# Second block's heads woven into a whole-fp32 projection, phase tables on VectorE in quarters, one order of products for both mixers

## The reference

```python
def first_block(...):                       # DEPTH = 2
    for l in range(DEPTH):
        h = rmsnorm(x, norm_mix[l])
        (u_ssm, q_lat, kv_lat, k_rope, hg_q, hg_f, hg_i, hg_g, gate_logits) = split(h @ w_in[l])
        y_ssm = s5_mixer(u_ssm, ...)        # complex state space scan: exp(lam*step)^t, B, C, gelu, GLU
        y_mla = mla_mixer(q_lat, kv_lat, k_rope, ...)
        y_hg  = hgrn2_mixer(hg_q, hg_f, hg_i, hg_g, ...)
        x = x + (gates[0]*y_ssm + gates[1]*y_mla + gates[2]*y_hg) @ w_out[l]
        x = x + memory_cross_attention(rmsnorm(x), rmsnorm(mem), ...)
        x = x + swiglu_ffn(rmsnorm(x), ...)
    return rmsnorm(x, norm_final)

def second_block(x, ...):                   # DEPTH = 2
    for l in range(DEPTH):
        h = rmsnorm_2(x, g_attn[l])
        qa, ka, va, qb, kb, vb = split(h @ w_in[l])      # w_in: 1024 x 2304
        qa, ka, qb, kb = rope(rmsnorm_2(each head))      # heads of 64
        ya = windowed_gqa_sink(qa, ka, va, sink[l])      # 8 heads, |distance| <= 128, a sink logit each
        yb = diff_attention(qb, kb, vb, lam)             # 4 heads: softmax(1) - lam * softmax(2)
        yb = rmsnorm_2(yb, subln[l]) * (1.0 - lambda_init)
        x = x + concat([ya, yb]) @ w_out[l]
        gate, val = split(rmsnorm_2(x, g_ffn[l]) @ w_up[l])
        x = x + (silu(conv3(gate)) * val) @ w_down[l]
    return x
```

## Time and profile before

| | us |
|---|---|
| median of three runs (2083.47 to 2090.02) | 2086.99 |
| the profiled execution, its own time | 2090.09 |
| its span in the trace | 2088.3 |
| PE busy | 1856.7 |
| DVE busy | 1269.5 |
| ACT busy | 919.5 |
| POOL busy | 311.8 |

### The profile page before, as it was taken

The page is one execution under the profiler, slowest core; times in us unless marked ns, Lnnn a source line. Parts: engine busy times, 40 slices in busy tenths (PEclk is TensorE's granted clock), DMA queues, the critical chain, the costliest instruction groups (busy, mean ns, idle before and its releaser), DMA issues.

```text
span 2088.3 us, 26733 instructions
## 1 busy us (share of the span) xinstructions
PE 1856.7 (89%) x9901; PEld 1469.5 (70%) x9901; DVE 1269.5 (61%) x1881; ACT 919.5 (44%) x1454; POOL 311.8 (15%) x253
## 2 busy tenths in 40 slices
PE   7899998876999989999888999767899988689998
PEld 6654556666997746556577998654699876368987
DVE  7883544548555494445455546797466669846665
ACT  3313334452346212334355445535455554446554
POOL 5000012049000000003011000540300026130000
PEclk9899999998999999999999999987799999779999
DMA  5344442442555334444053665430265544115654
GB/s 169 102 121 131 130 143 71 155 107 80 175 176 173 109 94 141 135 127 161 31 181 110 184 185 186 129 114 1 81 182 182 169 144 131 41 57 157 187 165 143
DMA packets 186262, 274.59 MB, mean 131 GB/s; under 512 B 25672, under 2 KB 121396, under 8 KB 186132
## 3 DMA queue, kind: packets, MB, share of 16 engines
q1 hardware_dynamic: 185268, 269.86, 42.1%
q0 software_dynamic: 864, 3.02, 0.5%
HBM read 271.78 MB, written 1.05 MB: 131 GB/s over the span
## 4 chain that ended last, share of the span: by engine, by line
PE 75%; DVE 15%; ACT 5%; issue 3%; POOL 1%; DMA 0%; DVEq 0%; ACTq 0%; POOLq 0%
PE bank L354 42%; PE bank L352 24%; DVE WL L940 2%; PE bank L462 2%; PE bank L483 1%; PE bank L560 1%; ACT XN L1221 1%; DVE TB L2097 1%; DVE NMX L1706 1%; DVE HRSTD L1681 1%; PE bank L900 1%; DVE SMALL L1679 1%; PE bank L731 1%; DVE TB L2123 1%; DVE A L2116 1%
## 5 line engine op out<-in xcount | busy, mean ns | idle before, releaser
L1181 ACT ACTIVATE WH<-W 128x1024 fp32r<-128x1024 f32 (+1 forms) x368 | 387.3, 1052 | 475.4 <-PE bank L354 419.4
L940 DVE TENSOR_TENSOR WL<-W,WH 128x1024 fp32r<-128x1024 f32 x288 | 384.9, 1336 | 295.7 <-ACT WH L1181 293.9
L354 PE MATMUL bank<-HTH,WH 128*128 128x256 f32 x1536 | 441.3, 287 | 21.4 <-DVE WL L940 18.9
L354 PE MATMUL bank<-HTL,WH 128*128 128x256 f32 x1536 | 439.0, 286 | 0.0
L354 PE MATMUL bank<-HTH,WL 128*128 128x256 f32 x1536 | 438.8, 286 | 0.0
L354 PEld LDWEIGHTS bank<-HTH,WH 128*128 128x128 f32 x1536 | 299.4, 195 | 24.4 <-DVE WL L940 16.3
L354 PE MATMUL bank<-WH,HTH 128*128 128x512 f32 (+1 forms) x704 | 282.5, 401 | 22.9 <-DVE HTL L1660 10.8
L354 PEld LDWEIGHTS bank<-HTL,WH 128*128 128x128 f32 x1536 | 299.6, 195 | 0.5 <-issue 0.5
L354 PEld LDWEIGHTS bank<-HTH,WL 128*128 128x128 f32 x1536 | 299.3, 195 | 0.0
L354 PE MATMUL bank<-WL,HTH 128*128 128x512 f32 (+1 forms) x704 | 277.7, 394 | 0.0
L354 PE MATMUL bank<-WH,HTL 128*128 128x512 f32 (+1 forms) x704 | 277.1, 394 | 0.0
(11 more groups left out here) (358 smaller groups left out, 2268.3 us busy)
## 6 DMA issues: line engine op xcount, KB each, us to landing
W<-in_w_in SPq DMA_DIRECT2D x128, 512.0 KB, 3.6
W<-in_ffn_w_gate_up SPq DMA_DIRECT2D x176, 256.0 KB, 3.2
W<-in_w_up SPq DMA_DIRECT2D x176, 256.0 KB, 3.2
W<-in_ffn_w_down SPq DMA_DIRECT2D x44, 512.0 KB, 3.3
W<-in_w_down SPq DMA_DIRECT2D x44, 512.0 KB, 3.6
W<-in_w_out SPq DMA_DIRECT2D x32, 512.0 KB, 4.1
W<-in_ssm_w_glu SPq DMA_DIRECT2D x16, 512.0 KB, 3.6
W<-in_x_w_kv SPq DMA_DIRECT2D x16, 512.0 KB, 3.4
```

Source lines behind the costliest of these rows:

```text
L354: m = pe.matmul(out, at_a(a[x]), at_b(b[y]), start=(start and i == 0), stop=(stop and i == 2), skip_group_check=True)
L940: eng.tensor_tensor(WL[:, m % HSLOTS, 0:width], W[:, n % RSLOTS, 0:width], h, ALU.subtract)\
L1181: copy = lambda dst, src, scale=1.0: act.activation(dst, src, ACT.Copy, scale=scale)
```

## The change

1. `w_in_2`'s projection uses whole products: `norm_cols` writes `HT2` (fp32), no parts of the weight are made. Products 3 and 4 are steps between window heads, and `wo2` steps lie between differential heads.
2. Window scores get their band mask on PE (a constant added by an fp32r matmul), maxima and exponentials read PSUM, the head scale is folded into the gains, and the division by the sum moves behind the value product, for all eight heads at once. Window outputs have tokens on partitions and are transposed after.
3. `begin` skips banks whose group is still open.
4. Phase tables of both layers are made by DVE, a quarter at a time; ACT takes the sines by quarters. Layer 1: quarters 0 and 1 in `aff_low` of layer 0's FFN, one piece a step, 2 and 3 at the start of its mixer.
5. Both layers' mixers use layer 1's order of products, except that `ssm_out(0..2)` of layer 0 come one product later.

```diff
 def begin(*name):
-    n = done["n"]
+    while done["n"] % BANKS in unfinished:
+        done["n"] += 1
...
+def window_scores(h):
+    r = 64 * (h % 2)
+    ps = begin("a2", "s", (l, h))
+    for tt in range(TT):
+        pe.matmul(ps[:, tt * S:tt * S + S], qkT[r:r + 64, h // 2, tt * P:tt * P + P],
+                  qkT[r:r + 64, 4 + h // 4, :], start=(tt == 0), stop=False, skip_group_check=True)
+    for tt in range(TT):
+        c = tt * S + (1 - tt) * P
+        m = pe.matmul(ps[:, c:c + P], IDENTR[:, :], BANDR[:, tt, :], start=False, stop=(tt == TT - 1), ...)
+def window_out(h):
+    freed("a2", "t", (l, h))
+    for tt in range(TT):
+        if h == 0: begin("so", l, tt)
+        for kt in range(TT):
+            m = pe.matmul(ps[:, h * HD:h * HD + HD], t_buf("a2", h)[:, kt, tt * P:tt * P + P],
+                          proj2[:, kt, 640 + (h // 4) * HD:640 + (h // 4) * HD + HD], ...)
...
-for j in range(5):
-    token_out(("p2", l, j), "w_in_2", l, HT, KT, 512 * j, 512 if j < 4 else 256, low="pool")
-    ...                                   # qk_T(0) after j == 2, qk_T(1) after j == 3, then 16 maps
+for j in range(3):
+    for _ in proj(j):                     # whole products of HT2
+        pass
+    if j == 1:
+        qk_T(0, (0, 1))
+qk_T(1, (2, 3))
+for j in range(3):
+    freed("qk2", l, j)
+pe.wait_ge(sem["band_high"], 1)
+rest = itertools.chain(proj(3), proj(4, kstep=4))
+for h in range(SWQ):
+    window_scores(h)
+    next(rest, None)
+    if h >= 1:
+        window_probs(h - 1)
+    if h >= 2:
+        window_out(h - 2)
+qk_T(2, (4, 5)); window_probs(SWQ - 1); window_out(SWQ - 2); qk_T(3, (6,))
+for j in range(3, 7):
+    freed("qk2", l, j)
+diff_scores(0); diff_scores(1)
+window_out(SWQ - 1)
+diff_scores(2); diff_scores(3)
+...                                       # waits for window_norm, transposes ya (two banks)
+diff_probs(0)
+mix = wide_steps(("wo2", l), "w_out_2", l, HT, 8, low="pool")
+for g in range(DFH):
+    if g < 2:
+        diff_scores(2 * g + 4); diff_scores(2 * g + 5)
+    if g == 0:
+        for j in range(2): freed("yaT", l, j)
+    next(mix)
+    if g == DFH - 1:
+        for i in range(2): freed("do", l, i)
+        out_T("ybT", ybt, 0)
+    diff_out(g)
+    if g < DFH - 1:
+        diff_probs(g + 1)
+freed("ybT", l, 0); next(mix); next(mix)
+for i in range(2, DFH): freed("do", l, i)
+out_T("ybT", ybt, 1); freed("ybT", l, 1)
+for _ in mix: pass
...
 # VectorE, phases (was: 16 multiplications, then four operations of 4096 columns)
+def phases(l, q):
+    part = slice(4 * q, 4 * q + 4)
+    c, n = cosT[:, part, :], sinT[:, part, :]
+    for j in range(4):
+        ins = ts_(c[:, j, :], TIME[:, :], th, None, ALU.mult)
+        ...                               # yield after every second
+    link(ts_(n, c, MAGIC, MAGIC, ALU.add, ALU.subtract)); yield
+    link(tt_(n, c, n, ALU.subtract)); yield
+    signal(stt(c, n, 0.25, n, ALU.is_gt, ALU.subtract), "phases", 4 * l + q + 1)
...
 # VectorE, second mixer
+for u in range(2): ...                    # norm_rope(0), norm_rope(1)
+rest = itertools.chain(norm_rope(2), norm_rope(3))
+for h in range(SWQ):
+    max_of(h)
+    next(rest, None)
+max_of(SWQ); max_of(SWQ + 1); window_norm(); max_of(SWQ + 2); max_of(SWQ + 3); diff_mix(0)
+for j in range(2): low_of(2 * j, 2, "yaT", l, j)
+max_of(SWQ + 4); max_of(SWQ + 5); diff_mix(1); max_of(SWQ + 6); max_of(SWQ + 7)
+diff_norm(0); diff_mix(2); diff_norm(1); diff_mix(3); low_of(4, 2, "ybT", l, 0)
+diff_norm(2); diff_norm(3); low_of(6, 2, "ybT", l, 1)
...
 # ScalarE, once before the second block's squares
+act.wait_ge(sem["band"], 1)
+link(copy(IDENTR[:, :], IDENT[:, :]))     # and two copies of the mask's band
 # PE, first mixer: was two orders by layer
+around(hf, 0); around(hq, 1)              # each: one chunk, ssm_in, the other chunks
+if l: ssm_out(l, 0); ssm_in(l, 2)
+mixer_tokens("hi", 2336)
+...                                       # layer 0: ssm_out 0, ssm_in 2; layer 1: ssm_out 1, ssm_in 3
+mixer_tokens("hg", 2848)
+if l == 0: ssm_out(l, 1); ssm_in(l, 3)
+for _ in kv: pass
+if l: ssm_out(l, 2)
+for _ in ql: pass
+ssm_out(l, 3 if l else 2)
```

More of the change, by code:

```diff
@@ L919, in _ @@
+                freed("ybT", l, 0)
+                next(mix)
+                next(mix)
+                for i in range(2, DFH):
+                    freed("do", l, i)
+                out_T("ybT", ybt, 1)
+                freed("ybT", l, 1)
                 for _ in mix:
@@ L1376, in take_hg @@
                         evict(HG[:, tt, :], "hg", l, tt, func=ACT.Silu)
+                if l == 0:
+                    for q in range(2):
+                        tables(l, q)
+                else:
+                    for q in range(4):
+                        tables(l, q)
                 for j in range(2):
@@ L1540, in _, with take_proj @@
                 nrm += 1
-                for j in range(5):
+                def take_proj(j):
                     for tt in range(TT):
@@ L1574, in _, with take_qk, out_squares @@
-                for j in range(2):
-                    high_of(4 + 2 * j, 2, "ybT", l, j)
+                def take_qk(*js):
+                    for j in js:
+                        evict(two(qkT, j), "qk2", l, j)
+                def out_squares(g):
+                    full("do", l, g)
+                    ps = bank(("do", l, g))
+                    link(act.activation(SCR[:, 0:P], ps[:, 0:P], ACT.Square, accum_out=YSSQ[:, g, 0:1]))
+                    signal(act.activation(SCR[:, 0:P], ps[:, P:2 * P], ACT.Square, accum_out=YSSQ[:, g, 1:2]),
+                           "yb_sq", DFH * l + g + 1)
@@ L1885, in _ @@
                     lambda_sums()
+                else:
+                    for q in range(2, 4):
+                        for _ in phases(l, q):
+                            pass
                 def latent_rstd():
@@ L2178, in _ @@
+                max_of(SWQ + 4)
+                max_of(SWQ + 5)
+                diff_mix(1)
+                max_of(SWQ + 6)
+                max_of(SWQ + 7)
+                diff_norm(0)
+                diff_mix(2)
+                diff_norm(1)
+                diff_mix(3)
+                low_of(4, 2, "ybT", l, 0)
+                diff_norm(2)
+                diff_norm(3)
+                low_of(6, 2, "ybT", l, 1)
                 add_x("wo2", l)
```

469 lines of the change are left out of this document (251 added, 218 removed).

## The result

| | before | after |
|---|---|---|
| median, us | 2088.42 (4 runs, 2083.47 to 2090.02) | 2009.51 (4 runs, 2007.12 to 2012.48) |
| ratio to before | 1 | 0.9628, interval 0.9617 to 0.9639 |
| profiled execution, its own time | 2090.09 | 2007.12 |
| span in its trace | 2088.3 | 2005.3 |

A forecast was written before the change was run, and what follows sets the result against it. PE, busy 89% of the span, was taken as the bound, with DVE or POOL setting its pace elsewhere. Terms -29.7 - 4.5 - 25.8 - 22.8 = -82.8 us from the median 2087.0 gave 2004, range 1974 to 2038.

The forecast's parts named there:

- Layer 0's FFN, -29.7: Layer 0's FFN: taking layer 1's tables off POOL saves 29.7 us of the 36.3 us excess over layer 1's FFN.
- First mixer, -4.5: Layer 0's first mixer: stalls removed, two new late banks cost some back; -4.5 us, bounds -13 and +3.
- Layer 1's first mixer and FFN, 0: Layer 1's first mixer keeps its order, so 0; no change was forecast for its FFN.
- Second mixers, -25.8 and -22.8: Second mixers of layers 1 and 0: 143 us from first projection to last addition instead of 167.0.
- The waits as recorded: Second mixers: PE's waits at last heads, qk evictions, `diff_mix(0)`, `ybT` banks and small pieces, together put at 11 us.
- "Hidden" in the window loop: Second mixers' window loop: DVE's and ACT's work per head fits within PE's 6.2 us while a chunk lasts.
- The hits of POOL, 4 us a layer: Second mixers: POOL's low parts of `wo2` stop DVE two or three times in the chain; 4 us, bounds 0 and 17.
- Half clock in the join, 3 us: Second mixers: PE runs at half clock behind waits of 2 us and more, costing 3 us.
- 1 (everything hides, 1982): Whole kernel: no late banks, no half clock and no POOL hits in the mixers; about 1982 us, chance 0.14.
- 2 (paced by DVE and ACT): Second mixers: per-head handoffs stop PE, a mixer needs some 160 us instead of 143; 2038 us, chance 0.14.
- 3 (a hit at each `wo2` step): Second mixers: POOL stops DVE at every `wo2` step, 17 us a layer instead of 4; 2030 us, chance 0.10.
- 4: Second mixers' projections: whole products lose full clock, 61.8 us more a layer; slower than before, 2128 us, chance 0.02.

The follow-up runs named there:

- e1b: Changed kernel with layer 1's phases made by POOL again and their sines inside layer 0's FFN, as before the change: 2039.33 us, ratio 0.9779.
- e2b: Kernel before the change, without POOL's five phase operations for layer 1 (tables hold constants, ACT's sines stay): 2060.33 us, ratio 0.9880.
- e3b: Changed kernel with layer 0's first mixer in its old order of products, tables still by quarters: 2010.42 us, ratio 0.9641.
- e6: Changed kernel, but ACT makes no high parts of w_out ahead in the first six window heads: 2004.08 us, ratio 0.9605.
- e10: Changed kernel with the low parts of wo2 made by DVE instead of POOL: 2006.58 us, ratio 0.9608.
- e4b: Changed kernel with the second mixer's projection in split products again, low parts by POOL, still woven with the window heads: 2031.76 us, ratio 0.9743.
- e5: Changed kernel with projection products 3 and 4 made before the window heads instead of between them: 2034.30 us, ratio 0.9749.
- e7: Changed kernel, but the first mixer's kv and ql skip the bank of y(1) and take the next: 1995.34 us, ratio 0.9563.

## Why the prediction was right

*Layer 0's FFN, -29.7, measured -29.3.* Right, by its mechanism: e1b brings the 12 us low part and 29 us back, e2b takes 26.4 us out by removing nothing but POOL's work. What was kept in the sum (transposes, the bank of `CT`, 2 us for phases on DVE: 6.6 us over layer 1's FFN) measured 8.2 us over it. The sines' move cost nothing at the start of layer 1's mixer.

*First mixer, -4.5, measured -2.1.* The recorded terms give 9.5 + 5 - 11 = 3.5, not 4.5. The two late banks were found by counting `begin`, and both are in the trace with 3.24 and 3.32 us. The net is too small to be called measured: e3b is within its interval of after, and two executions of the same code differ by 2.8 us. What it missed: `uq` starts 6.2 us earlier than before (133.40, 139.62), but 2.6 of that are only the latent sums, which now come behind it, and from there to the last `ssm_out` PE needs 21.7 us (to 155.12), the sums' 2.6 among them, for the products that took 17.4 before (to 157.00). The other 1.7 us are half clock behind the sums' one-column products (granted clock 0.86 from 142.94 to 155.10), which the sum had nowhere.

*Layer 1's first mixer and FFN, 0, measured -1.9 and -1.1.* Not predicted. The code around them changed little, and the spread between executions is of that size.

*Second mixers, -25.8 and -22.8, measured -24.2 and -24.3.* 143 us from projection to last addition, found 142.6 and 144.3. The total is better than the terms. The waits as recorded (2, 2, 2.6, twice 2, 2) add up to 12.6 us, not 11; with that the sum would be 145.9. In layer 1 PE is idle 15.2 us, where 11 + 4 - 1 = 14 were forecast, and busy 129.1, where 126.3 + 3 = 129.3 were. Inside these:
- The band matmuls (0.28 us from one start to the next, 0.25 said), window outputs (0.93, 0.95) and the wait for `diff_mix(0)` (2.63, 2.6) were sized well. The two `ybT` waits are 0.65 and 1.54, where twice 2 was said.
- "Hidden" in the window loop was wrong: 2.93 us of bank wait and 2.4 of half clock from ACT's standing for `w_out`'s first chunks. I had counted ACT's work per head and not the transfers that its queue waits for. e6 removes both, and half of it or more comes back in later waits.
- The hits of POOL, 4 us a layer with bounds 0 and 17: three hits of 2 us were there as said. One of them held PE, for 2.3 us (3.11 us of wait, 0.80 in e10); what the other two cost is not shown by itself. The term was too large by up to 1.7 us.
- Half clock in the join, 3 us: PE's busy time is 2.8 us over its work at full clock. PE's clock is 0.90 and 0.95 in the last two stretches; by that a fifth of 33.0 and a tenth of 66.4 us lie at the 1.2 GHz level, 13 us, of which at most half is lost: 6.6. So the term lies between what was said and twice that.

So 2.9 us of idle time in the window loop that nobody forecast, the addition that was 1.6 short, and the `ybT` waits and the hits that were some 2 us too high each largely cancelled, and that is luck. The mechanism of the whole, PE's idle time and its clock, held. What the gain consists of I had not weighed: e4b is 11 to 12 us a layer slower without the whole products, e5 13.6 without the weaving (the two need not add up), and I took the weaving as idle time filled, where it is nearly all the clock.

*The rivals.* 1 (everything hides, 1982) was wrong for this kernel: both late banks of layer 0 are there, and so are the hits. e7 shows that one of the two is worth some 6 us, and layer 1's, which the rival left alone, as much. 2 (paced by DVE and ACT) and 3 (a hit at each `wo2` step) are out by 142.6 and 144.3 us. 4 is out by the clock of 0.98 in the projections. A hit lasts as long as POOL's instruction: 2.39 us on DVE beside 2.34 on POOL, both ending within 0.2 us (the prediction gave no row of POOL for its hit of 2.26 us; the low part beside it took 2.4 to 2.5). That is what the Trainium skill says for engines that share ports ("SBUF — State Buffer", "Who interferes with whom"); the traces agree.

## What to carry to other kernels

When one engine looks busy all the time, look at who stops it: a helper whose instructions hold another engine's (here POOL's held DVE's, 2 us at a time and once 11) may cost more than the work it takes over, and more work on PE (12.8 us here) can be the cheaper form. Count the banks and the DMA waits that stand in the queue of each helper engine, not its busy time, and price a PE wait of a few us at one to two times its length, because of the clock behind it (5.8 us for 3.32 and 6.6 for 5.83 in e7), less the next wait that takes its place (e6). A stretch of short dependent products is worth weaving into a stream of long ones even where PE shows 90% busy: read the granted clock of the stretch first.

## What the runs showed of the hardware

- Small products with waits between them ran at a granted clock of 0.64 while PE was busy 28.05 of 31 us (e5); the same products with half a projection between them at 0.90.
- A bank wait of 3.32 us was worth about 5.8 us in e7, one of 5.83 us 6.6: what a wait costs was not in proportion to its length.
- The same 2.87 us wait was followed by 1.10 us for 16 matmuls in one trace and by 1.96 us in another.
- While POOL worked on 4096 columns (14.02 us), a DVE operation of 1.24 us took 12.51; beside POOL's low parts of 2.4 us, DVE operations of 0.17 to 0.43 us took 2.1 to 2.5.
